# Attention with the query tiles mixed into it, sums of squares gathered on VectorE, and weights split by halves

## The reference

```python
y = xf * lax.rsqrt(jnp.mean(xf * xf, axis=-1, keepdims=True) + EPS)   # every norm
q = apply_rope(rmsnorm_2(q, q_gain), cos, sin)     # 16 heads of 64
k = apply_rope(rmsnorm_2(k, k_gain), cos, sin)     # 4 heads of 64
s = jnp.einsum('bqkgd,bskd->bkgqs', q_blk, k) * scale
p = jax.nn.softmax(s, axis=-1).astype(v.dtype)
return jnp.einsum('bkgqs,bskd->bqkgd', p, v)       # then @ w_o
```

## Time and profile before

| | |
|---|---|
| three runs | 3398.29, 3399.99, 3401.54 us |
| the profiled execution | 3402.33 us, its span 3400.1 us |
| mean granted TensorE clock | 0.948 of full speed |
| TensorE busy (matmul) | 91% |
| VectorE, ScalarE, GpSimd busy | 42%, 21%, 45% |
| DMA | 259.51 MB, mean 76 GB/s |

### The profile page before, as it was taken

The page is one execution under the profiler, slowest core; times in us unless marked ns, Lnnn a source line. Parts: engine busy times, 40 slices in busy tenths (PEclk is TensorE's granted clock), DMA queues, the critical chain, the costliest instruction groups (busy, mean ns, idle before and its releaser), DMA issues.

```text
span 3400.1 us, 38788 instructions
## 1 busy us (share of the span) xinstructions
PE 3083.2 (91%) x14739; PEld 2403.7 (71%) x14739; DVE 1417.6 (42%) x1983; ACT 720.1 (21%) x1069; POOL 1525.8 (45%) x926
## 2 busy tenths in 40 slices
PE   8897899999887999999989889999989777699998
PEld 7885898788634877788866437888867344478886
DVE  5675655111234047433344552332066666433311
ACT  2373222433232000111013551111011111011100
POOL 5441322444203655565543014666555444456663
PEclk9997999999898999999999999999989788899999
DMA  3110000222100245556541002333222000123331
GB/s 111 62 63 32 1 0 0 63 74 74 38 0 25 99 161 182 165 173 188 192 133 62 0 13 62 99 90 102 93 64 101 16 16 16 50 75 99 98 103 59
DMA packets 291644, 259.51 MB, mean 76 GB/s; under 512 B 6329, under 2 KB 263958, under 8 KB 291276
## 3 DMA queue, kind: packets, MB, share of 16 engines
q1 hardware_dynamic: 287840, 248.53, 23.4%
q0 software_dynamic: 2256, 6.55, 0.6%
q10 hardware_dynamic: 1436, 2.96, 0.2%
HBM read 255.92 MB, written 2.10 MB: 76 GB/s over the span
## 4 chain that ended last, share of the span: by engine, by line
PE 78%; DVE 9%; issue 4%; ACT 3%; POOL 2%; DVEq 2%; DMA 1%; POOLq 1%; ACTq 0%; SPq 0%
PE ps L487 19%; PE ps L488 19%; PE ps L489 18%; DVE cv L1881 2%; PE ps L1377 2%; PE ps L1357 2%; PE ps L1453 2%; PE ps L1150 1%; PE ps L1163 1%; PE ps L578 1%; PE ps L1260 1%; PE ps L1169 1%; PE ps L692 1%; DVE HN L598 1%; PE ps L1270 1%
## 5 line engine op out<-in xcount | busy, mean ns | idle before, releaser
L487 PE MATMUL ps<-HNH,spl 128*128 128x512 f32 (+1 forms) x2496 | 914.5, 366 | 61.3 <-DVE HNL L591 24.2
L661 POOL TENSOR_TENSOR spl<-raw,spl 128x1024 fp32r<-128x1024 f32 (+1 forms) x352 | 894.5, 2541 | 55.3 <-issue 5.5
L488 PE MATMUL ps<-HNL,spl 128*128 128x512 f32 (+1 forms) x2496 | 899.3, 360 | 0.0
L489 PE MATMUL ps<-HNH,spl 128*128 128x512 f32 (+1 forms) x2496 | 895.7, 359 | 0.0
L659 POOL CAST spl<-raw 128x1024 fp32r<-128x1024 f32 (+1 forms) x352 | 390.5, 1109 | 1055.0 <-PE ps L489 974.5
L487 PEld LDWEIGHTS ps<-HNH,spl 128*128 128x128 f32 x2496 | 480.2, 192 | 160.9 <-issue 58.6
L488 PEld LDWEIGHTS ps<-HNL,spl 128*128 128x128 f32 x2496 | 480.6, 193 | 72.6 <-issue 4.3
L489 PEld LDWEIGHTS ps<-HNH,spl 128*128 128x128 f32 x2496 | 479.4, 192 | 69.7
L487 PE MATMUL ps<-AFH,spl 128*128 128x512 f32 x528 | 212.8, 403 | 0.0
L489 PE MATMUL ps<-AFH,spl 128*128 128x512 f32 x528 | 205.8, 390 | 0.0
L488 PE MATMUL ps<-AFL,spl 128*128 128x512 f32 x528 | 205.8, 390 | 0.0
(11 more groups left out here) (419 smaller groups left out, 4348.9 us busy)
## 6 DMA issues: line engine op xcount, KB each, us to landing
adw<-in_ada_w SPq DMA_DIRECT2D x96, 512.0 KB, 6.2
raw<-in_w_in SPq DMA_DIRECT2D x44, 1024.0 KB, 5.2
raw<-in_ffn_w_up SPq DMA_DIRECT2D x88, 512.0 KB, 4.8
raw<-in_w_ffn_in SPq DMA_DIRECT2D x44, 512.0 KB, 5.0
raw<-in_ffn_w_down SPq DMA_DIRECT2D x16, 1408.0 KB, 6.4
raw<-in_hy_w_in SPq DMA_DIRECT2D x12, 1024.0 KB, 5.1
raw<-in_w_ffn_out SPq DMA_DIRECT2D x8, 1408.0 KB, 6.8
raw<-in_w_branch_dn SPq DMA_DIRECT2D x8, 1024.0 KB, 5.1
```

The source lines that it names most:

```text
L487: pe.matmul(dst, w[0], x[0], start=first, stop=False)
L488: pe.matmul(dst, w[0], x[1], start=False, stop=False)
L489: return pe.matmul(dst, w[1], x[0], start=False, stop=final)
L661: pool.tensor_tensor(lo, w, hi, ALU.subtract).then_inc(split_ready, 1)
```

## The change

Weights: `pool_split` splits the first half of a tile's input channels and then the second, four operations in place of two. TensorE tells after its first half (`acc_half`), so that GpSimd may overwrite that part, waits for `split_first` at the start of a tile and for `split_ready` at its middle.

Norms: ScalarE squares tile 0 and tile 7 into the two NSQ buffers and tiles 1 to 6 into PSUM banks 1 and 3; VectorE adds these six to the first buffer, and TensorE makes two fp32 matmuls, both after the product. Norm 0 is as it was.

Attention: keys, values and two query tiles come first; each of the other six is made in the loop, half of it in the second of four steps and half in the third. A step takes one tile of 128 queries of a pair of heads, the even one on partitions 0 to 63 and the odd one on 64 to 127, whose matmuls alternate in scores and in the product with the values. Probabilities of two steps are kept in place of two heads'. The loop is written out, and GpSimd's copies, the buffer OG and the copy into it (L1784) are gone. Low halves are taken from PSUM.

```diff
                 self.s0, self.u0, self.f0 = Gemm.slabs, 2 + 2 * Gemm.slabs, Gemm.evacs
                 self.turn = R if pair else 2 * R
+                self.mid = (kt + 1) // 2
                 Gemm.slabs += nslab
                 Gemm.evacs += nslab if pair else 2 * nslab
...
@@ -496,9 +495,11 @@
 
             t = 2 * r + m
             b = gm.buf(t)
-            pe.wait_ge(split_ready, i * (2 * R) + (gm.u0 + t + 1))
+            pe.wait_ge(split_first, i * (2 * R) + (gm.u0 + t + 1))
             pe.wait_ge(acc_free[b], i * (gm.turn // 2) + gm.free(t))
             for k in range(gm.kt):
+                if k == gm.mid:
+                    pe.wait_ge(split_ready, i * (2 * R) + (gm.u0 + t + 1))
                 if ready and t == 0:
                     pe.wait_ge(*ready(k))
                 w, tok = halves_of(gm, t, k), x(k)
@@ -508,6 +509,8 @@
                                       k == 0, k == gm.kt - 1)
                 else:
                     mm = products(pe, ps[:, 2 * b, :], w, tok, k == 0, k == gm.kt - 1)
+                if k == gm.mid - 1:
+                    mm.then_inc(acc_half, 1)
...
             return ap.unsqueeze(1).broadcast_to([ap.shape[0], n, ap.shape[1]])
 
         gq_k = Gemm(w_cols(A["attn_w_qkv_2"][0], QH * HD), 1, KD)
+        gq_v = Gemm(w_cols(A["attn_w_qkv_2"][0], (QH + KVH) * HD), 1, KD)
         gq_q = Gemm(w_cols(A["attn_w_qkv_2"][0], 0), 4, KD)
         GQ_TILES = [(gq_k, t, KD + t) for t in range(2)] + [(gq_q, t, t) for t in range(KD)]
-        gq_v = Gemm(w_cols(A["attn_w_qkv_2"][0], (QH + KVH) * HD), 1, KD)
+        PAIRS, FIRST_Q, AHEAD = QH // 2, 2, 4
+        STEPS = PAIRS * NT
+
+        def late_tile(e):
+            n = AHEAD + e // NT
+            return n if n < len(GQ_TILES) else None
         gq_out = Gemm(w_cols(A["attn_w_o_2"][0], 0), 4, KD)
...
-                if k >= 2:
-                    act.wait_ge(n_sum, KD * u + k - 1)
-                act.activation(NSQ[:, k % 2, 0:n], x(k), ACT.Square).then_inc(n_sq, 1)
-            act.wait_ge(n_sum, KD * (u + 1))
+                if u:
+                    if k in (3, 4, 5, 6):
+                        act.wait_ge(n_add, (KD - 2) * (u - 1) + k - 2)
+                    dst = NSQ[:, k // (KD - 1), 0:n] if k in (0, KD - 1) else ps[:, 1 + k % 2 * 2, 0:n]
+                    act.activation(dst, x(k), ACT.Square).then_inc(n_sq, 1)
+                else:
+                    if k >= 2:
+                        act.wait_ge(n_sum, k - 1)
+                    act.activation(NSQ[:, k % 2, 0:n], x(k), ACT.Square).then_inc(n_sq, 1)
+            act.wait_ge(n_sum, KD + 2 * u)
...
+        def norm_pe(pe, u):
+            pe.wait_ge(n_add, (KD - 2) * u)
+            pe.matmul(ps[:, 6, :], ones[:, :], NSQ[:, 0, 0:SEQ], start=True, stop=False).then_inc(n_sum, 1)
+            pe.wait_ge(n_sq, KD * (u + 1))
+            pe.matmul(ps[:, 6, :], ones[:, :], NSQ[:, 1, 0:SEQ], start=False, stop=True).then_inc(n_sum, 1)
+
+        def norm_add(dve, u, k):
+            dve.wait_ge(n_sq, KD * u + k + 1)
+            dve.drain()
+            x = NSQ[:, 0, 0:SEQ]
+            dve.tensor_tensor(x, x, ps[:, 1 + k % 2 * 2, :], ALU.add).then_inc(n_add, 1)
...
@@ -654,11 +678,17 @@
                     if r not in seen:
                         pool.wait_ge(slot_full[gm.slot(r)], i * (16 * gm.parts * R // 2) + gm.full(r))
                         seen.add(r)
+                    w, hi, lo = gm.view(r)[:, :, m * P:(m + 1) * P], gm.half(u, 0), gm.half(u, 1)
+                    first, second = slice(0, gm.mid), slice(gm.mid, gm.kt)
+                    old = acc_ready if gm.kt > KD and i == 0 and u < 2 else acc_half
+                    pool.wait_ge(old, i * (2 * R) + (gm.u0 + u - 1))
+                    pool.tensor_copy(hi[:, first, :], w[:, first, :])
+                    pool.drain()
+                    pool.tensor_tensor(lo[:, first, :], w[:, first, :], hi[:, first, :], ALU.subtract).then_inc(split_first, 1)
                     pool.wait_ge(acc_ready, i * (2 * R) + (gm.u0 + u - 1))
-                    w, hi, lo = gm.view(r)[:, :, m * P:(m + 1) * P], gm.half(u, 0), gm.half(u, 1)
-                    pool.tensor_copy(hi, w)
+                    pool.tensor_copy(hi[:, second, :], w[:, second, :])
                     pool.drain()
-                    pool.tensor_tensor(lo, w, hi, ALU.subtract).then_inc(split_ready, 1)
+                    pool.tensor_tensor(lo[:, second, :], w[:, second, :], hi[:, second, :], ALU.subtract).then_inc(split_ready, 1)
...
-            def stage_qk(g):
-                pool.tensor_copy(qst[:, :, :], QG[:, ds(g * 2, 2), :]).then_inc(a_qk, 1)
-                pool.tensor_copy(kst[:, :].unsqueeze(1), KDUP[:, ds(g, 1), :]).then_inc(a_qk, 1)
...
+                pool_split(pool, gm)
 
...
+            def qk_sum(n):
+                pe.wait_ge(h_sq, 2 * HEADS + n + 1)
+                if n >= AHEAD:
+                    taken(pe, gq_q, 0, GQ_TILES[n][1])
+                    bank = 7
+                else:
+                    pe.wait_ge(h_rs, 2 * HEADS + n + 1)
+                    bank = 6
+                pe.matmul(ps[:, bank, :], pair_ones, NSQ[:, n % 2, 0:SEQ], start=True, stop=True).then_inc(h_sum, 1)
...
+            def q_part(n, bank, ks):
+                gm, t, _ = GQ_TILES[n]
+                if ks[0] == 0:
+                    pe.wait_ge(split_first, gm.u0 + t + 1)
+                    if n < AHEAD:
+                        pe.wait_ge(acc_free[gm.buf(t)], gm.free(t))
+                    else:
+                        pe.wait_ge(a_done, n)
+                for k in ks:
+                    if k == gm.mid:
+                        pe.wait_ge(split_ready, gm.u0 + t + 1)
+                    mm = products(pe, ps[:, bank, :], halves_of(gm, t, k), x_hn(k), k == 0, k == KD - 1)
+                    if k == gm.mid - 1:
+                        mm.then_inc(acc_half, 1)
+                if ks[-1] == KD - 1:
+                    mm.then_inc(acc_ready, 1)
...
+            def scores(e):
+                p, q = e // NT, e % NT
+                if q == 0:
+                    pe.wait_ge(a_done, FIRST_Q + p + 1)
+                if e >= 2:
+                    pe.wait_ge(a_e, 2 * (e - 1))
+                for s in range(2):
+                    x = slice(s * HD, (s + 1) * HD)
+                    mm = pe.matmul(ps[:, e % 2 * 2 + s, :], QG[x, p, q * P:(q + 1) * P], KDUP[x, p // 2, :], start=True, stop=True)
+                mm.then_inc(a_s, 1)
+
+            def turn_over(e):
+                for s in range(2):
+                    i = 2 * e + s
+                    pe.wait_ge(a_p, i + 1)
+                    if i >= 2:
+                        pe.wait_ge(a_tc, i - 1)
+                    for kt in range(NT):
+                        mm = pe.transpose(ps[:, 4 + s, kt * P:(kt + 1) * P], PB[:, e % 2, s, kt * P:(kt + 1) * P], ident)
+                    mm.then_inc(a_t, 1)
+
+            def weighted(p):
+                pe.wait_ge(a_tc, 2 * NT * (p + 1))
+                if p:
+                    pe.wait_ge(split_x, NT + KD + p)
+                for kt in range(NT):
+                    for s in range(2):
+                        x = slice(s * HD, (s + 1) * HD)
+                        mm = pe.matmul(ps[x, 6, :], VG[:, kt, p // 2 * HD:(p // 2 + 1) * HD], PTB[:, p % 2, s, kt, :],
+                                       start=kt == 0, stop=kt == NT - 1)
+                mm.then_inc(a_o, 1)
+
+            n_ready = lambda k: (n_out, 2 * KD + k + 1)
             for t in range(2):
-                pe_tile(pe, gq_v, 0, 0, t, x_hn)
-                if t == 0:
-                    qk_rot(9)
+                pe_tile(pe, gq_k, 0, 0, t, x_hn, ready=n_ready)
+            qk_sum(0)
+            pe_tile(pe, gq_v, 0, 0, 0, x_hn)
+            qk_sum(1)
+            qk_rot(0)
+            pe_tile(pe, gq_v, 0, 0, 1, x_hn)
+            qk_rot(1)
+            k_dup(0)
+            q_part(2, 2 * gq_q.buf(0), range(KD))
+            k_dup(1)
+            k_dup(2)
+            q_part(3, 2 * gq_q.buf(1), range(4))
+            qk_sum(2)
+            k_dup(3)
+            q_part(3, 2 * gq_q.buf(1), range(4, KD))
+            qk_rot(2)
             pe.wait_ge(a_dupc, KVH)
             for t in range(2):
-                taken(pe, gq_v, 0, t)
-                for c in range(NT):
-                    mm = pe.transpose(ps[:, 4 + t, c * P:(c + 1) * P], NSQ[:, t, c * P:(c + 1) * P], ident)
-                mm.then_inc(sv_t, 1)
...
-            pe.wait_ge(a_oc, 2 + QH // 2)
-            pe_gemm(pe, gq_out, lambda k: (OGH[:, k, :], OGL[:, k, :]), lambda k: (split_x, NT + KD + k + 1), tile_after=norm_after(pe, 3))
+            for e in range(STEPS):
+                p, j, n = e // NT, e % NT, late_tile(e)
+                if e + 2 < STEPS:
+                    scores(e + 2)
+                if j == 0 and p:
+                    weighted(p - 1)
+                if n and j in (1, 2):
+                    q_part(n, 7, range(4 * j - 4, 4 * j))
```

(133 more changed lines are left out.)

252 lines of the change are left out of this document (61 added, 191 removed).

## The result

The median is 3295.01 us (four runs, 3294.09 to 3299.15) against 3399.14 of the kernel before in the same runs: a ratio of 0.9696, interval 0.9679 to 0.9713. The profiled execution took 3295.33 us, its span 3293.5. The direction was right and the size wrong: 3317 was predicted, and the time lies under the range's low end of 3302. In the profiled executions the gain is 107.0 us where 83 were worked out, so 24 us are to be explained (by the span, 106.6 and 23.6).

The account below looks back on a forecast made before the run. TensorE, busy 91% of the span, was taken as the bound. 3402.3 less 31 for norms, 6 for splits and 46 for attention gave 3319.3, as a median 3317; the range went from 3302 to 3357.

Parts of the forecast that it names:

- low end of 3302: Whole kernel: lower end of the range, with the largest norm and split terms and no collisions.
- Rivals 2 and 3: Attention steps one at a time, 3409 us; GpSimd bounding the products, 3423 us; chance 0.03 together.
- 31 worked out: Norms: six fp32 matmuls of 0.86 us go in each of 6 norms, 31.0 us less; ends 26 and 32.
- The first rival: Attention: no overlap on the array, each record keeps its 0.43 us; 3351 us as a median, chance 0.25.
- a pair of scores is 3 x 0.43 + 0.2 = 1.5 us: Attention scores: with overlap on the array a pair takes 1.5 us, in series 1.9.
- 9 x 0.43 + 0.1 = 4.0: Attention, product with the values: eight matmuls of a pair of heads take 4.0 us, in series 7.0.
- the wait for the rotation: Attention loop: the next query tile waits for VectorE's rotation, 3.1 us of which 2.4 are covered.
- the turn of 22.3: Attention loop: four steps that make a late query tile take 22.3 us, in series 26.6.
- the loop of 163.8: Attention: the whole loop, from first four steps to the closing copy and values, takes 163.8 us, in series 196.4.
- The 3 us for collisions: Attention loop: 3 us lost to splits that fall on VectorE's work; ends 0 and 12.
- in the steady state nothing is to be had: Splits by halves: a split of 3.6 us already fits a tile of 5.5, so no gain there.
- The three starts for which 6 us were taken: Products beginning with nothing split, at 610.74, 1076 and 2949: 1.4 us less, about 3 at 1076, together 6.

Follow-up runs that it names:

- norms alone: The kernel before with only the norm's sums changed: 3365.89 us, ratio 0.9895.
- halves alone: The kernel before with only the split by halves and its waits: 3383.87 us, ratio 0.9948.

## Why the prediction was right in kind and wrong in size

**What bounds the kernel: right.** Where TensorE's work was taken out the end came sooner by as much. Rivals 2 and 3, one step in flight and GpSimd as the bound, did not happen: the new loop has waits of about a microsecond, and TensorE waits for GpSimd in places only.

**Norms: right.** 31 worked out, 35.3 measured alone, and 33.0 in the six stretches of that trace. The additions are 0.69 us as taken. In the branch's output product a wait of 2.35 us went as well, which the term did not have.

**Overlap on the array: right, and too small.** The first rival (3351) fell. The step that failed is "a pair of scores is 3 x 0.43 + 0.2 = 1.5 us". It let only the second record of one matmul run beside the first of the next. The trace has four records start as two pairs, 1.06 us. With 32 pairs that is 14 us at most. For the values "9 x 0.43 + 0.1 = 4.0" measured 3.58, by the same cause. Against that the wait for the rotation was 1.2 instead of 0.7. So the first four steps took 14.9 instead of 16.7, the turn of 22.3 was 20.6, the two fours without a late tile 15.8 and 13.0 instead of 16.4 and 14, and the loop of 163.8 was 152.3, which is 11.5 us of the 24. Ahead of the loop 46 was worked out and 46.7 measured. The 3 us for collisions were not spent (0), and the first tile, which "the change leaves", cost 2.3 more. The balance of the attention is 57.5 instead of 46, and the loop is all of that miss.

**Halves: the cause that was missed.** The step that failed is "in the steady state nothing is to be had". It looked at TensorE's tile of 5.5 us against a split of 3.6 and left out who else stands beside GpSimd. In the convolution stage VectorE's operations wait for whole subtractions; with shorter ones the scan starts 9.5 us sooner. The three starts for which 6 us were taken gave 1.5 each; the 3 us for the one beside VectorE were too many, and behind it 3.2 were lost, with the two waits shown above. A fourth start, near 1263, isn't in the term: TensorE waits there for VectorE's low halves (6.42 us before, 3.77 after), and the stretch gained 2.65. The stretches with splits alone gave 13 instead of 6: 7 of the 24.

**The remaining 5 us** are the norm stretches, 36.1 instead of 31. The traces of the parts divide them: in these six stretches norms alone gained 33.0 and halves alone 3.1. So 2 are the sum's, with the wait that went, and 3 are the halves', which the prediction gave nothing here.

**The range.** Its low end of 3302 is said to take the largest norm and split terms and no collisions. Those are 1, 3 and 3 us and give 3310; the other 8 have no term. It had no price for a pair below 1.5 us, though the prediction itself named half of the serial time as the other bound. With the pair at 0.86, half of the serial time of its four records, and the values at 3.5, five turns alone are 5 x (4 x 0.64 + 0.5) = 15 us shorter. That puts the low end at 3287 and the measured time inside; from 3310 it is 3295, just the measured time.

## What to carry to other kernels

Price neighbours on disjoint halves of the array at half of their serial time, and put that value at the range's end when no row shows such a pair. For an operation of GpSimd ask not only whether it fits its own slot but how long it is, since a VectorE operation on SBUF that meets it waits for its end; where VectorE sets the pace, shorter operations can pay even if they make GpSimd busier. Move the short producer of a wait (here one matmul of 0.9 us) in front of independent work before giving it a price.

## What the runs showed of the hardware

- fp32 matmuls, two records each, pair completely on disjoint halves: four records in 1.06 us on halves of the rows, sixteen in 3.58 on halves of the columns, against 0.43 us a record in series. The Trainium skill ("TensorE: Matmul & The Clock Gate", section "Measured speedup vs the span model") reports gains of this kind, 3.07 times for four row tiles; here two tiles give 1.6 for the scores, with the change of form in it, and 1.9 for the values.
- TensorE pairs across a longer order too: with the even head's matmuls all ahead of the odd head's, sixteen records still took 5.35 us instead of 6.9.
- The blocking of GpSimd and VectorE is paid per operation, in both directions. A convolution operation of 0.77 us took up to 2.66 beside whole subtractions and up to 1.55 beside halves. A half subtraction of 1.26 us took 3.12 when it began inside VectorE's 128x2048 subtraction and a whole one of 2.34 took 4.20: 1.86 us more in either case, since 2.0 us of VectorE's operation were left in both. Two halves pay it twice.
- The norm's additions, which read one of their inputs from PSUM, don't wait: all 36 take 686 to 690 ns, though 19 of them begin inside an operation of GpSimd.
- The same split is a gain where VectorE is late and a loss where GpSimd is.
